# A two-block transformer kernel on Trainium2: slots three blocks later, fetched rows one a block, a third pair of buffers

## The reference, cut to what matters

```python
def chunk(xc):
    q = (xc @ w_query).reshape(PEER_TOKEN_CHUNK, PEER_HEADS, 2, PEER_HALF)
    s1 = jnp.einsum('thd,hnd->thn', q[:, :, 0], sub_keys_1).astype(jnp.float32)
    s2 = jnp.einsum('thd,hnd->thn', q[:, :, 1], sub_keys_2).astype(jnp.float32)
    v1, i1 = lax.top_k(s1, PEER_TOPK)
    v2, i2 = lax.top_k(s2, PEER_TOPK)
    ...
    best, pos = lax.top_k(cand, PEER_TOPK)
    idx = jnp.take_along_axis(cand_idx, pos, axis=-1)
    g = jax.nn.softmax(best, axis=-1)
    u = expert_u[idx]
    act = jax.nn.gelu(jnp.einsum('td,thkd->thk', xc, u).astype(jnp.float32), approximate=False)
    w = (g * act).astype(h.dtype)
    return jnp.einsum('thk,thkd->td', w, expert_v[idx])
```

## Time and profile before

| | before |
|---|---|
| median of three executions | 1282.47 us |
| the profiled execution | 1282.63 us |
| its span, first to last instruction | 1281.2 us |
| TensorE busy | 1220.8 us (95%) |
| VectorE busy | 1037.7 us (81%) |
| ScalarE busy | 679.3 us (53%) |
| mean granted clock of TensorE | 0.991 of full |
| block 0 starts | 634.45 us |
| last matmul of block 127 starts | 1271.66 us |

### The profile page before, as it was taken

The page is one execution under the profiler, slowest core; times in us unless marked ns, Lnnn a source line. Parts: engine busy times, 40 slices in busy tenths (PEclk is TensorE's granted clock), DMA queues, the critical chain, the costliest instruction groups (busy, mean ns, idle before and its releaser), DMA issues.

```text
span 1281.2 us, 26843 instructions
## 1 busy us (share of the span) xinstructions
PE 1220.8 (95%) x11398; PEld 1031.1 (80%) x11398; DVE 1037.7 (81%) x1612; ACT 679.3 (53%) x969; POOL 313.0 (24%) x202
## 2 busy tenths in 40 slices
PE   6899888999999999999999899999999999999997
PEld 5545774888844546648999799999999989999996
DVE  4865884899956766677899789999998888989884
ACT  5663231767635435646545456776665444545553
POOL 0322221144500000000113500000004556555640
PEclk9999998999999999999999899999999999999999
DMA  7530003755566332457536656555459999999981
GB/s 292 201 107 26 2 2 132 288 206 198 205 223 250 107 103 95 139 190 259 203 132 232 214 198 219 182 194 198 171 193 336 341 337 357 358 339 402 338 315 34
DMA packets 51352, 266.44 MB, mean 208 GB/s; under 512 B 5136, under 2 KB 5408, under 8 KB 32544
## 3 DMA queue, kind: packets, MB, share of 16 engines
q1 hardware_dynamic: 40192, 226.76, 49.5%
q0 software_dynamic: 10160, 35.96, 7.5%
q10 hardware_dynamic: 880, 1.99, 0.5%
HBM read 262.04 MB, written 2.10 MB: 206 GB/s over the span
## 4 chain that ended last, share of the span: by engine, by line
PE 62%; DVE 22%; issue 6%; DMA 5%; ACT 4%; ACTq 0%; DVEq 0%; POOL 0%; POOLq 0%
PE bank L680 18%; PE bank L686 18%; PE bank L683 18%; DMA arena<-in_expert_rows,arena 5%; PE bank L1109 2%; DVE ring L2159 2%; DVE ring L2295 2%; DVE X L2159 2%; DVE arena L2336 1%; PE bank L760 1%; DVE arena L2309 1%; DVE arena L2159 1%; DVE ring L1793 1%; DVE arena L2298 1%; DVE HT L2159 1%
## 5 line engine op out<-in xcount | busy, mean ns | idle before, releaser
L680 PE MATMUL bank<-arena 128*128 128x256 f16 (+3 forms) x720 | 216.4, 307 | 0.6 <-DVE arena L1463 0.4
L683 PE MATMUL bank<-arena 128*128 128x256 f16 (+3 forms) x720 | 216.3, 307 | 0.0
L686 PE MATMUL bank<-arena 128*128 128x256 f16 (+3 forms) x720 | 216.2, 307 | 0.0
L1463 DVE SCALAR_TENSOR_TENSOR arena<-ring,arena 128x2048 f16<-128x2048 f32 (+1 forms) x59 | 133.9, 2273 | 31.8 <-ACT arena L2511 31.7
L3223 POOL DMA_INDIRECT arena<-in_expert_rows,arena x32 | 72.7, 2272 | 285.5 <-PE bank L686 236.2
L680 PE MATMUL bank<-cst,arena 128*128 128x224 f16 (+2 forms) x544 | 133.3, 254 | 0.4 <-DVE arena L1463 0.4
L686 PE MATMUL bank<-cst,arena 128*128 128x224 f16 (+2 forms) x544 | 133.3, 254 | 0.0
L683 PE MATMUL bank<-cst,arena 128*128 128x224 f16 (+2 forms) x544 | 133.3, 254 | 0.0
L2511 ACT ACTIVATE arena<-ring 128x2048 f16<-128x2048 f32 (+1 forms) x59 | 111.2, 1892 | 28.9 <-PE bank L686 28.9
L2959 ACT CAST arena<-arena 128x448 f16<-128x448 f32 x64 | 36.0, 565 | 138.3 <-PE bank L686 138.3
L2159 DVE SCALAR_TENSOR_TENSOR X<-ring,X 128x2048 f16<-128x2048 f32 x42 | 96.2, 2290 | 14.2 <-ACT X L2904 14.1
(11 more groups left out here) (379 smaller groups left out, 3660.8 us busy)
## 6 DMA issues: line engine op xcount, KB each, us to landing
ring<-in_expert_u SPq DMA_DIRECT2D x64, 1024.0 KB, 4.8
ring<-in_expert_v SPq DMA_DIRECT2D x64, 1024.0 KB, 8.5
ring<-in_w_in_n SPq DMA_DIRECT2D x24, 1024.0 KB, 4.8
ring<-in_w_up_t SPq DMA_DIRECT2D x22, 1024.0 KB, 4.8
ring<-in_w_down_n SPq DMA_DIRECT2D x11, 1024.0 KB, 4.8
ring<-in_w_out_n SPq DMA_DIRECT2D x8, 1024.0 KB, 4.8
ring<-in_w_query_t SPq DMA_DIRECT2D x8, 1024.0 KB, 4.8
ring<-in_w_in_t SPq DMA_DIRECT2D x3, 1024.0 KB, 7.0
```

The lines of the kernel that those rows point to most:

```text
L680: pe.matmul(out_, stat[0], mov[0], start=start, stop=False, skip_group_check=shared)
L683: pe.matmul(out_, stat[0], mov[1], start=False, stop=False, skip_group_check=shared)
L686: return pe.matmul(out_, stat[1], mov[0], start=False, stop=stop, skip_group_check=shared)
L1463: nv.scalar_tensor_tensor(out=lo, in0=ld.slot(i), scalar=W_UP, in1=hi, op0=ALU.mult, op1=ALU.subtract).then_inc(s["split_lo"], 1)
```

## The change

Three things change. `SLOTS_AFTER` goes from (11, 29) to (14, 29): `slots(0)` stands behind block 14 instead of block 11, while the place of `slots_evicted(0)` in VectorE's program stays. The tables of rows: rows in were five in four blocks, from block 64 to block 89, and are now one a block, from block 64 to block 95; rows out were one a block, from 91 to 122, and are now one a block from 96 to 126, with two at block 110; the gelu moves from block 90 to block 95. And the halves of the weights get a third pair of buffers, in space that held one-hot vectors before: `w_hi(n)` waits for weights n-3, and is issued three blocks ahead instead of two, with one more at the start.

```diff
-SLOTS_AFTER = (11, 29)
+SLOTS_AFTER = (14, 29)
...
-ROWS_IN = [max(0, min(NG, 5 * (n - 63) // 4)) for n in range(128)]
-ROWS_OUT = [max(0, min(NG, n - 90)) for n in range(128)]
-ROW_GELU = 90
+ROWS_IN = [max(0, min(NG, n - 63)) for n in range(128)]
+ROWS_OUT = [max(0, min(NG, n - 95 + (n >= 110))) for n in range(128)]
+ROW_GELU = 95
...
+    m.Wh, m.Wl = (w_ + [f16(t[:, at:at + 256], 2, 256)] for w_, at in ((m.Wh, 33280), (m.Wl, 33536)))
...
-                               (m.Wh[q % 2][:, j, 0:NT], m.Wl[q % 2][:, j, 0:NT]), (q, j, odd) == (0, 0, 0),
+                               (m.Wh[q % 3][:, j, 0:NT], m.Wl[q % 3][:, j, 0:NT]), (q, j, odd) == (0, 0, 0),
...
     def w_hi(n):
-        if n >= 2:
-            na.wait_ge(s["v_done"], n - 1)
-        na.copy(m.Wh[n % 2][:, :, 0:NT], m.answers[:, 2 * n:2 * n + 2, :]).then_inc(s["w_hi"], 1)
+        if n >= 3:
+            na.wait_ge(s["v_done"], n - 2)
+        na.copy(m.Wh[n % 3][:, :, 0:NT], m.answers[:, 2 * n:2 * n + 2, :]).then_inc(s["w_hi"], 1)
...
     for q in range(64):
-        if q + 2 < 64:
-            w_hi(q + 2)
+        if q == 0:
+            w_hi(2)
+        if q + 3 < 64:
+            w_hi(q + 3)
```

More of the change, by code:

```diff
@@ L2326, in w_lo @@
         nv.wait_ge(s["w_hi"], n + 1)
-        nv.tensor_tensor(m.Wl[n % 2][:, :, 0:NT], m.answers[:, 2 * n:2 * n + 2, :], m.Wh[n % 2][:, :, 0:NT],
+        nv.tensor_tensor(m.Wl[n % 3][:, :, 0:NT], m.answers[:, 2 * n:2 * n + 2, :], m.Wh[n % 3][:, :, 0:NT],
                          ALU.subtract).then_inc(s["w_lo"], 1)
```

## The result

The changed kernel takes 1269.53 us (median of five, 1268.91 to 1270.83) against 1282.47 us (five, 1280.68 to 1283.20) of the kernel before on the same chip: ratio 0.9901, 95% interval 0.9888 to 0.9915. On another chip, later, it was 1270.83 us, ratio 0.9899 (0.9883 to 0.9916). The forecast was 1269.5 us. The profiled execution has a span of 1268.2 us, 13.0 less than before.

What follows compares the result with a forecast made beforehand. TensorE, busy 95% of the span, was taken as the bound, so only its waits could be gained: -7.74 (slots) - 5.75 (rows) + 0.5 (end) = -13.0 us, from 1282.47 to 1269.5 us; range 1267.6 to 1273.0 for 8 in 10.

Steps and rivals of the forecast that it cites:

- Slots: Blocks 18 and 19: moving the slots three blocks later removes 7.74 us, 6.24 of wait and 1.50 of lower clock.
- Rows one a block: Blocks 73 to 89: with fetches three blocks ahead, VectorE's waits for rows go and TensorE gains 5.75 us.
- the step for the third pair: ScalarE writes weights' high halves a block earlier; VectorE only idles later, 0 in blocks 66 to 125.
- Double row: Block 110's two rows: VectorE waits about 1.1 us, then some 0.5 in blocks 111 and 112; TensorE loses 0.
- The end: Row 31 in the last iteration delays the rows' sums; cost 0.5 us, bounds from -0.4 to 4.4.
- The bounds for a late fetch: At the end: cost 1.6 us if row 31's fetch takes 10.0 us, 4.4 if it takes 12.8.
- 1: Fetches stay the bound, landing after 12.8 us everywhere from block 64 on; loses 6.3 us, 1275.8 us; chance 6%.
- 2: The slots' stall returns at the second tile's naming, block 30; if all 6.24 us return, 1275.7 us; chance 5%.
- 3: DMA as a whole bounds blocks from 64 on; at 310 GB/s a block takes 5.07 us, 1298.6 us; chance 3%.
- 4, the backlog: Final inputs' backlog stays, fetches take 12.8 us at the double row and the end; +0.5 and +3.9, 1273.9 us; 5%.

Runs made afterwards that it cites:

- e4: The changed kernel with the slots behind block 12 instead of 14; 1271.31 us, ratio 0.9901 to the kernel before.
- e2: The kernel before with only the tables of rows and the gelu's block changed, slots and two pairs of buffers as before; 1278.56 us, ratio 0.9957.
- e3: The kernel before with only the third pair of buffers added, slots and tables as before; 1276.69 us, ratio 0.9946.
- e9: The changed kernel with an unused VectorE addition of two SBUF inputs (448 columns) behind each row in blocks 64 to 123; 1272.77 us, one execution.
- e6: The changed kernel with a second double row, at block 118, so no row stands in the last iteration; 1268.49 us, ratio 0.9883 to the kernel before.
- e1: The kernel before with only the slots moved, behind block 14, tables and two pairs of buffers as before; 1275.12 us, ratio 0.9929.
- e11: The kernel before with one VectorE reordering, the row's turn ahead of the weights' low half in blocks 64 to 127; 1277.90 us, ratio 0.9966.
- e10: The changed kernel with an unused one-input VectorE sum over 448 columns behind each row in blocks 64 to 123; 1270.79 us, one execution.
- e7: The changed kernel with old row tables, second tile's slots after block 30, weights 0 ahead of the matrix's low half in block 63; 1267.44 us, ratio 0.9873.

## Why the prediction was right

The sum, -13.0 us, is what was measured, and each term stands at its place in the table. One step behind it was wrong and showed in no stretch: what the third pair does.

- **Slots.** Right in the place (no wait for L2277), the size (-7.74) and the split into wait and clock (e4). The lead of block 22, 4.34 us, is the forecast's 4.4.
- **Rows one a block.** The size was right, -5.76. The mechanism holds for the table by itself (e2). In the whole change it is not the only cause: the step for the third pair failed, "without it VectorE only idles later, before the matrix's low half", and from that "0 in blocks 66 to 125". The first half of it is what happened; that the place of the idling is free was wrong. Measured alone the pair takes the same 5.75 us (e3), and the two don't add, since there was only one stall to take away. That a part worth 5.75 us could be priced at 0 and the sum still come out is luck: the table, priced rightly, had already taken the whole stall. The landing of 9.7 us that I carried over from the earlier trace rows became 6.9: that row was not a property of the DMA alone, but of what VectorE runs while the fetch is issued.
- **Double row.** A wait of 0.63 us instead of 1.1, none of 0.5 behind it, nothing lost by TensorE: right, with more to spare than reckoned, by the shorter landing. With the landings of 11 us in e9 the same row waited 2.48 us.
- **The end.** +0.72 against +0.5; the wait before the sums is 1.10 us. By e6 the row in the last iteration costs 1.1 us, where the forecast had 0.9; the weights made earlier give back 0.4 (tail 21.64 against 22.04 before), as forecast. The bounds for a late fetch left out the clock, which was 1.7 of the 3.8 us that e9 lost there.
- **Rivals.** 1 is out: no fetch of the first pass lands after 7.5 us (9.4 in the second profile), and in the second pass, with one of 12.1 us, the median is 8.2. 2 is out by e1. 3 is out: blocks 64 to 126 go at 4.60 us but for the one ahead of 104. 4, the backlog, is the one that came nearest, and not where I looked: not on fetches but on the load of one matrix (17.8 us), at block 104, where VectorE's lead fell to 0.68 us. The loads' backlog cleared as the earlier trace rows said (loads issued from 1143 to 1164 us landed after 7.4 to 8.7 us), and for 80 us 349 GB/s were moved with no wait of TensorE. I had read the lead at the double row and at the end, and not at the slowest load, which the earlier trace rows show too.

Open: in e9's second pass the issue mostly is not let in where the filler ends (0.19 us after it began, in the lines above) nor where the low half does, but at the third end, 0.89 us before it is over. Five issues beside the same instructions, also without a gap, were let in at the first, and in e11 one was too. What tells them apart, these runs don't say.

## What to carry to other kernels

An edit priced at nothing "because the engine only idles elsewhere" needs a look at who works during that idle time: here, with the same table of rows, the kernel whose VectorE rests behind the row has no stall (e3), and the one where it rests in front of the weights has 5.75 us of it (before). Two parts that each remove the same stall don't add, so a right sum says nothing on which of them did it; only one-part kernels do, and here they say that for this stretch a reordering of two instructions would have done. Before a duration of a gather is carried over, check what VectorE runs beside its issue, and count the lead at the slowest load, not only where the change adds work.

## What the runs showed of the hardware

- The issue of an indirect fetch of 128 rows takes 0.94 us on GpSimd where VectorE rests or runs e10's one-input instruction when it starts. Otherwise it ended, in 422 of 442 cases, 0.8 to 1.0 us after the end of the Vector instruction that was running: 1.08 us in all beside a short one (128x448), 1.68 beside a row, 2.75 or 2.88 beside a low half (128x2048). 17 of e9's took 3.81.
- The landing follows: 6.9 us instead of 9.7 at the median of the first pass; within e9's second pass 8.0 beside 11.1.
- This loops back: when VectorE is late it has no rest behind a row, its fetches are issued more slowly, and the next row can come later still (e7 around 1064 us, the kernel before in blocks 74 to 90).
- A wait of TensorE of 1.5 us left the granted clock at 1.00; one of 6.1 us was followed by a block at 0.74. Two waits, of 1.8 and 1.3 us with 1.3 us of work between them (e9), were followed by matmuls at half the clock (0.50 from 1251 to 1253 us).
- What lies ahead of block 0 differs by up to 2.4 us between profiles of kernels that are the same there (block 0 starts at 633.50 to 635.87), while blocks 0 to 20 take 92.33 us in each of the nine profiles with the slots behind block 14. Differences of a few us are to be read from stretches, not from ends.
